# First scores ahead of the last natural values, gate weights beside the ring, values' first chunks split during the gates

## The chip, the cores and the metric

The kernel runs on one core of one Trainium2 chip. The metric is the device time of one execution, in microseconds. Three executions of the kernel before took 2294.04 to 2295.73 us, median 2295.2.

## The reference, cut to what matters

All arithmetic is float32. A first block runs 256 tokens of width 1024 through two layers. Each projects the normalised tokens and feeds four kinds of attention of four heads each: stick-breaking (`sb`), block attention with a relative bias (`mb`), a native sparse attention of three branches (`cmp` on 15 compressed blocks, `slc` and `win`) with sigmoid gates, and differential attention (`df`). A second block adds 256 context tokens, a matrix LSTM and a latent attention of eight heads, each followed by a convolutional feed-forward. Cut to what the change touches:

```
proj = rmsnorm(x) @ w_in                       # queries, keys ("proj"); values, gates ("nat")
kc, vc = (gelu(blocks(t) @ w1) @ w2 for t in (k_c, v_c))    # "hid": the hidden rows of the compression
for each head unit: o = softmax(q @ k.T * scale + bias) @ v
o_nsa = g0 * o_cmp + g1 * o_slc + g2 * o_win;  x = x + concat(o) @ w_out
...
x_m = h @ w_up; x_c = silu(dwconv(x_m)); gates = x_c @ w_gates + b; v = x_m @ w_v   # mLSTM
q = rope(rms(h @ w_dq) @ w_uq); o = softmax(q @ k.T * s) @ v @ w_out                # latent attention
```

## The kernel before, in words

Every engine has an instruction list written out by hand, and semaphores tie them. One list of 1 MB slots (128 x 2048 floats) holds all large weights in their order of use. SyncE loads them into a ring of two slots (`load`, `load_span`); slot w is issued when `slot_done` counts w - 1, that is when the slot before the last has been split.

A product in float32 is made of three products of rounded parts. ScalarE copies a slot of weights into the rounded type (L1309, two halves), VectorE subtracts to get the rest (L1789, two halves, `slot_done`). The same is done to each chunk of 128 input rows (L1333 or L1331 on ScalarE, L1814 or L1811 on VectorE). TensorE then does three products for each output tile (`linear`, L793; L798 where the input is stationary, "natural"). `feed_to(q)` splits all chunks up to q and the weight slots that they need, and one slot ahead; `ws` holds two split slots and `xs` four 256-column cells. So ScalarE and VectorE stay a little ahead of TensorE. Where one of them has other work in its list at that time, TensorE waits.

Results go to eight PSUM banks, given out in turn by `ticket_plan`. A ticket waits until the copy of the ticket eight turns before has freed its bank (`bank_free`).

**Attention of the first block, in each of the two layers.** After the projections, TensorE does the first six of eight natural chunks, the hidden rows of the compression (L943, 128 small products), the last two natural chunks, and four small transposes (L953). Then comes a loop over p = 0 to 15, a pipeline of three steps. In step p TensorE does the scores of pair p (L1005, L1007; 14 pairs of head units), one or two units of the modulation (L965), the transposes of the weights of pair p - 2 (L1048; L1044 for `cmp`) and their products with the values (L1077, L1079). VectorE makes the logits and their maxima (L1945 to L1948; L1936, L1938 for `sb`) and normalises pair p - 1 (L2012 to L2025, which releases the transposes). ScalarE takes the exponentials (L1464, L1465; L1448 to L1454 and L1470 for `sb`) and copies the transposed weights out (L1442). In layer 0 eight transposes of the context tokens (L1031) stand in each of the steps 0 and 1, and ScalarE copies them out (L1475). The natural results are copied out by ScalarE (L1411 to L1415) ahead of the loop; TensorE's scores of pairs 1 and 2 take the banks that these copies free. At p = 0 VectorE makes the gelu's argument (L1953 to L1963), ScalarE its exponential at p = 1 (L1427), VectorE the rest (L1979 to L1983). At p = 7 (`OUT_X_AT`) ScalarE and VectorE split the first four chunks and the second weight slot of the output projection. The loop ends in `linear(out)`.

**mLSTM.** Four groups `m_up` end in the convolution and its silu, then 32 products for the gates (L1127, straight from the ring slot, not split), then 14 filler products on constants (`keep_warm`, L866), then four groups of values `m_v` (16 chunks each, natural). VectorE adds the gates' bias (L2106, L2108, which also counts `slot_done`), ScalarE makes a logarithm of the sigmoid (L1568 to L1572), and VectorE runs six scans (L2122 to L2126) with chunks of the first group fed between them. When the scans' result is ready, four transposes (L1138) follow the first group, and ScalarE copies them out (L1587) behind that group's four results (L1583).

**Latent attention.** In a loop over i, one of 16 score tiles each (L1238, L1239), TensorE transposes tile i - 2 (L1247) and multiplies with the values for each head (L1257). VectorE rotates two heads' queries in each of the first four steps (L2345 to L2348), which frees the banks that the score tiles take, reduces the maximum (L2381) and normalises the tile before (L2387, L2389, which releases the transposes). At i = 1 it splits the first slot of the output projection.

Of the kernel before, what the change touches and what calls it, by code (L numbers as in the profile page):

```python
# [42 lines left out]
OUT_X_AT = 7  # L43
# [92 lines left out]
NP = NU // 2  # L136

# [111 lines left out]
def stream_plan():  # L249
# [11 lines left out]
    w.direct("m_gates")  # L261
# [22 lines left out]
def ticket_plan():  # L284
# [3 lines left out]
    for l in range(DEPTH):  # L288
# [6 lines left out]
        n.add(("hid", l))  # L295
        n.add(("hidT", l))
        for p in range(NP + 2):
            if p < NP:
                n.add(("S", l, 2 * p), 1)
                n.add(("S", l, 2 * p + 1), 1)  # L300
# [3 lines left out]
            if l == 0 and p < 2:  # L304
                n.add(("xC", 2 * p))
                n.add(("xC", 2 * p + 1))
# [89 lines left out]
def G(*name):  # L396
    return ST.g[name if len(name) > 1 else name[0]]
# [13 lines left out]
def build(nc, tokens, stream, side, params, params1, consts, onehot, out, scratch):  # L411
    with ExitStack() as ctx:
# [109 lines left out]
        mv = region(o("v"), (4, MH * T2))  # L522
        mqk = region(o("qk"), (4, T2))
# [36 lines left out]
        late_full = [sem(f"late_side_full{i}") for i in range(2)]  # L560
        conv_ready = sem("conv_ready")
# [110 lines left out]
        def _(sp):  # L672
# [77 lines left out]
            load_span(at, ST.n)  # L750
# [8 lines left out]
        def _(pe):  # L759
# [156 lines left out]
            for l in range(DEPTH):  # L916
# [29 lines left out]
                linear(G("nat", l), 6)  # L946
# [7 lines left out]
                ins.then_inc(bank_full[n % BANKS], 1)  # L954

                for n in range(N(("proj", l, 1)), N(("proj", l, 1)) + 4):
                    pe.wait_ge(bank_free[n % BANKS], n // BANKS + 1)
# [31 lines left out]
                for p in range(NP + 2):  # L989
                    if p < NP:  # L990

                        two = [(UNITS[i], N(("S", l, i))) for i in (2 * p, 2 * p + 1)]
                        if two[0][0]["kind"] == "cmp":
                            for n in (N(("kc", l)), N(("vc", l))):
                                pe.wait_ge(bank_free[n % BANKS], n // BANKS + 1)
                        for u, n in two:
                            pe.wait_ge(bank_free[n % BANKS], n // BANKS)
                        for t in range(2):
                            for u, n in two:
                                f = slice(u["r"], u["r"] + u["kk"])  # L1000
                                rows_q = qk[f, u["q"], t * P:t * P + P]
                                if u["kind"] == "cmp":
                                    ins = mm(ps(n, 16 * t, 16 * t + 16), rows_q, kcT[f, :], start=True, stop=True)
# [4 lines left out]
                                if t == 1:  # L1008
                                    ins.then_inc(bank_full[n % BANKS], 1)
# [1584 lines left out]
```

## Time and profile before

| | |
|---|---|
| median of three executions | 2295.2 us |
| profiled execution | 2294.72 us, span 2292.9 us |
| TensorE busy, of the span | 2210.5 us (96%) |
| VectorE, ScalarE busy | 1340.3 us (58%), 1183.8 us (52%) |
| mean granted TensorE clock | 0.99 of 2.4 GHz |
| read from memory | 309.11 MB, 135 GB/s |

PE is TensorE's products and PEld its weight loads, DVE is VectorE, ACT ScalarE, SPq SyncE's queue. A timeline row gives start and duration in us, engine, line, operation, output and inputs, how many, and in brackets the idle time of the engine before and what ended it. Durations of pipelined products overlap, and some records can be missing. In rows of windows each engine has its busy time and its number of instructions, then come the granted clock (1.00 is 2.4 GHz, 0.50 is 1.2 GHz), the DMA share and GB/s.

### The profile page before, as it was taken

What the parts mean: (1) busy time and instruction counts of PE and PEld (TensorE: products, weight loads), DVE (VectorE), ACT (ScalarE), POOL (GpSimd) and SP (SyncE); (2) the same over time, 40 slices, a digit from 0 to 9 for tenths busy, and PEclk for the clock granted to TensorE, in tenths of its full rate; (3) what the DMA queues carried; (4) which work ended last, traced back from release to release, by engine and by line L of the source; (5) the groups of instructions that cost most, each with busy time, mean ns of one, the idle gap of its engine ahead of it and who ended that gap; (6) DMA issues with size and microseconds to landing.
All of it is one profiled execution on the core that took longest, in us unless ns stands there. A gap on an engine that the chain in (4) does not pass through costs nothing.

```text
span 2292.9 us, 33613 instructions
## 1 busy us (share of the span) xinstructions
PE 2210.5 (96%) x13542; PEld 1831.2 (80%) x13542; DVE 1340.3 (58%) x2204; ACT 1183.8 (52%) x2002; POOL 0.2 (0%) x4
## 2 busy tenths in 40 slices
PE   8989999979999999999999999999999998999998
PEld 8659989849999777787677676868888877668998
DVE  6776645685654655445667664356666436546764
ACT  4665535575544564444344443257555337447764
POOL 0000000000000000000000000000000000000000
PEclk9999999989999999999999999999999999899999
DMA  8735575753576213222222121222222222214542
GB/s 311 269 134 182 216 302 201 281 199 120 178 291 258 92 56 110 92 92 92 74 74 70 68 83 37 92 74 92 97 106 92 92 92 92 92 42 154 182 168 99
DMA packets 45719, 312.28 MB, mean 136 GB/s; under 512 B 4951, under 2 KB 7255, under 8 KB 8580
## 3 DMA queue, kind: packets, MB, share of 16 engines
q1 hardware_dynamic: 45572, 310.20, 37.3%
q8 instruction: 107, 1.75, 0.3%
q14 instruction: 40, 0.33, 0.0%
HBM read 309.11 MB, written 1.07 MB: 135 GB/s over the span
## 4 chain that ended last, share of the span: by engine, by line
PE 84%; DVE 9%; ACT 5%; issue 1%; DMA 0%; ACTq 0%; DVEq 0%; SPq 0%
PE bank L793 63%; PE bank L798 9%; DVE ws L1789 2%; PE bank L965 2%; ACT ws L1309 2%; PE bank L1195 1%; DVE xs L1814 1%; PE bank L1166 1%; PE bank L1239 1%; DVE hT L1945 1%; PE bank L1257 1%; PE bank L1238 1%; PE bank L866 1%; PE bank L1127 1%; DVE arena L2216 1%
## 5 line engine op out<-in xcount | busy, mean ns | idle before, releaser
L793 PE MATMUL bank<-xs,ws 128*128 128x256 f32 (+1 forms) x9648 | 1569.0, 323 | 26.5 <-DVE xs L1814 15.3
L793 PEld LDWEIGHTS bank<-xs,ws 128*128 128x128 f32 x9648 | 1396.5, 190 | 204.3 <-issue 34.1
L1789 DVE TENSOR_TENSOR ws<-ring,ws 128x1024 fp32r<-128x1024 f32 x462 | 545.5, 1222 | 293.3 <-ACT ws L1309 293.2
L1309 ACT ACTIVATE ws<-ring 128x1024 fp32r<-128x1024 f32 x462 | 462.7, 1049 | 300.3 <-PE bank L793 195.0
L1814 DVE TENSOR_TENSOR xs<-arena,xs 128x512 fp32r<-128x512 f32 (+1 forms) x286 | 162.5, 581 | 287.2 <-ACT xs L1333 285.8
L1333 ACT ACTIVATE xs<-arena 128x512 fp32r<-128x512 f32 (+1 forms) x286 | 149.2, 539 | 332.4 <-PE bank L793 221.8
L798 PE MATMUL bank<-ws,xs 128*128 128x512 f32 (+1 forms) x1008 | 230.0, 388 | 5.7 <-ACT arena L1587 2.2
L798 PEld LDWEIGHTS bank<-ws,xs 128*128 128x128 f32 x1008 | 188.5, 189 | 45.8 <-DVE ws L1789 2.6
L1333 ACT ACTIVATE xs<-hT 128x512 fp32r<-128x512 f32 (+1 forms) x216 | 123.0, 573 | 196.9 <-PE bank L793 187.9
L1814 DVE TENSOR_TENSOR xs<-hT,xs 128x512 fp32r<-128x512 f32 (+1 forms) x216 | 133.5, 620 | 155.5 <-ACT xs L1333 155.4
L1811 DVE SCALAR_TENSOR_TENSOR xs<-xT,par,xs 128x256 fp32r<-128x256 f32 x112 | 51.2, 480 | 11.9 <-ACT xs L1331 11.8
L1331 ACT ACTIVATE xs<-xT,par 128x256 fp32r<-128x256 f32 x112 | 51.9, 495 | 7.3 <-DVE xT L1829 7.3
L965 PE MATMUL bank<-arena,cs 128*32 128x256 f32 x768 | 55.5, 409 | 0.0
L1343 ACT ACTIVATE arena<-xT 128x512 f32<-128x512 f32 (+1 forms) x52 | 28.5, 563 | 36.5 <-DVE xT L2267 26.7
L1537 ACT ACTIVATE arena<-bank,par 128x512 f32<-128x512 f32 (+1 forms) x60 | 41.6, 693 | 9.9 <-PE bank L793 9.9
L866 PE MATMUL bank<-con 128*128 128x256 f32 x202 | 46.4, 382 | 0.0
L866 PEld LDWEIGHTS bank<-con 128*128 128x128 f32 x202 | 38.2, 192 | 8.0 <-issue 3.2
L1195 PE MATMUL bank<-arena 128*128 128x512 f32 (+1 forms) x128 | 42.7, 488 | 0.1
L2076 DVE SCALAR_TENSOR_TENSOR arena<-arena,par 128x510 f32<-128x510 f32 (+1 forms) x60 | 38.9, 648 | 3.3 <-ACT arena L1556 3.3
L2078 DVE SCALAR_TENSOR_TENSOR arena<-arena,par 128x510 f32<-128x510 f32 (+1 forms) x60 | 39.2, 653 | 2.1
L1048 PE MATMUL bank<-con,hT 128*128 128x128 f32 x144 | 24.1, 302 | 15.3 <-DVE hT L2025 12.6
L1195 PEld LDWEIGHTS bank<-arena 128*128 128x128 f32 x128 | 24.1, 190 | 18.3 <-issue 15.3
(259 smaller groups left out, 1364.3 us busy)
## 6 DMA issues: line engine op xcount, KB each, us to landing
ring<-in_stream SPq DMA_DIRECT2D x233, 1024.0 KB, 4.8
arena<-in_side SPq DMA_DIRECT2D x56, 1024.0 KB, 5.0
arena<-bias_vectors SPq DMA_DIRECT2D x1, 1536.0 KB, 9.0
hT<-in_tokens SPq DMA_DIRECT2D x1, 1024.0 KB, 5.0
arena<-in_tokens SPq DMA_DIRECT2D x1, 1024.0 KB, 12.7
out<-arena SPq DMA_DIRECT2D x2, 512.0 KB, 3.1
arena<-in_params SPq DMA_DIRECT2D x1, 918.0 KB, 8.2
arena<-bias_vectors SPq DMA_DIRECT2D x1, 706.0 KB, 10.5
```

The lines of the kernel that those rows point to most:

```text
L793: ins = mm(ps(n, c, c + g.T), a[wi][:, p * P:(p + 1) * P], x[xi], start=first, stop=last)
L798: ins = mm(ps(n, 0, width), x[xi][:, (p // nh) * P:(p // nh + 1) * P], a[wi][:, (p % nh) * 512:(p % nh) * 512 + width], start=first, stop= ...
L866: mm(ps(n, at, at + cols), ones, con[:, 0:cols], start=True, stop=True)
L965: ins = mm(bank[n % BANKS][c:c + 32, 0:T], cs[:, k, 2 * ADA_B - 2 - 2 * u:2 * ADA_B + 30 - 2 * u], wd[:, k, :], start=(u == 0 and k < 4), ...
L1195: ins = mm(ps(n, T_AT[st_], T2), mv[:, st_, h * T2 + e * P:h * T2 + (e + 1) * P], mP[:, 0, OFF[st_]:OFF[st_] + T2 - T_AT[st_]], start=(st_ ...
L1309: do(ws[:, i % 2, 0, c], ring[:, w % R, c], ACT.Copy).then_inc(w_high, 2 // halves_in)
L1331: do(split_x(q, 0), source(g, k), ACT.Identity, scale=par_at(g.gain, k)).then_inc(x_high, 1)
L1333: do(split_x(q, 0), source(g, k), ACT.Copy).then_inc(x_high, 1)
L1537: return do(dst, ps(n, 0, cols), ACT.Identity, scale=w[:, 1:2], bias=b)
L1789: ins = v.tensor_tensor(ws[:, i % 2, 1, c], ring[:, w % R, c], ws[:, i % 2, 0, c].bitcast(F32), ALU.subtract)
L1811: stt(split_x(q, 1), source(g, k), par_at(g.gain, k), split_x(q, 0).bitcast(F32), ALU.mult, ALU.subtract).then_inc(x_done, 1)
L1814: v.tensor_tensor(split_x(q, 1), source(g, k), split_x(q, 0).bitcast(F32), ALU.subtract).then_inc(x_done, 1)
```

## The change

In the attention loop the scores of pair 0 move ahead of the last two natural chunks, and the four small transposes go between these two chunks. ScalarE takes the exponentials of pair 0, of lambda and of the gelu ahead of the natural copies. The gates of the sparse attention are finished at VectorE's step 3 in place of step 1. The context's transposes move from steps 0 and 1 to 1 and 2. `OUT_X_AT` becomes 14. In the mLSTM the gates' weights leave the stream: a DMA of 1 MB brings them into a free part of the arena once `m_up` group 0 is done; it stands in SyncE's list between the loads of the stream. ScalarE and VectorE split chunks 0 and 1 of the first values (and the slot after) ahead of their work on the gates, the 14 fillers go, and the transposed gate rows are copied out ahead of the first group's results. In the latent attention VectorE's split of the output projection's first slot moves from i = 1 to i = 6.

```diff
-OUT_X_AT = 7
+OUT_X_AT = NP                                   # 14
-    w.direct("m_gates")                         # stream_plan
@@ ticket_plan
         n.add(("hid", l))
+        n.add(("S", l, 0))
+        n.add(("S", l, 1))
         n.add(("hidT", l))
         for p in range(NP + 2):
-            if p < NP:
+            if 0 < p < NP:
...
-            if l == 0 and p < 2:
-                n.add(("xC", 2 * p))
+            if l == 0 and 1 <= p <= 2:
+                n.add(("xC", 2 * p - 2))
@@ sync
-            load_span(at, ST.n)
+            load_span(at, ST.w[("m_up", 2)])
+            n = N(("m_up", 0), 3)
+            sp.wait_ge(bank_full[n % BANKS], n // BANKS + 1)
+            sp.dma_start(gate_weights, side[DEPTH * SIDE_W]).then_inc(gates_full, 16)
+            load_span(ST.w[("m_up", 2)], ST.n)
@@ tensor
-                linear(G("nat", l), 6)
+                for n in range(N(("proj", l, 1)), N(("proj", l, 1)) + 4):
+                    pe.wait_ge(bank_free[n % BANKS], n // BANKS + 1)
+                scores(0)                       # the score products of step p, now a function
+                linear(G("nat", l), 6, 7)
                 n = N(("hidT", l))
...
                     ins = nc.tensor.transpose(ps(n, 16 * i, 16 * i + 16), hrow[:, i, :], ident[0:16, 0:16])
                 ins.then_inc(bank_full[n % BANKS], 1)
+                linear(G("nat", l), 7)
...
-            pe.wait_ge(slot_full[(W("m_gates")) % R], 16 * ((W("m_gates")) // R + 1))
-            wd = slot(W("m_gates"), MK)
+            pe.wait_ge(gates_full, 16)
+            wd = gate_weights.rearrange("p (k n) -> p k n", k=MK)
...
-            keep_warm(N("m_aT"), T, T, 14)
@@ scalar
                 feed(G("nat", l))
+                for i in range(2):
+                    softmax_exp(i)              # waits logits_ready; the two Exp of a pair's unit
+                act_.wait_ge(lam_sum, seen(lam_sum))
+                do(lam[:, 2:4], lam[:, 0:2], ACT.Exp).then_inc(lam_exp, 1)
+                act_.wait_ge(gelu_arg, l + 1)
+                do(hid, hidg, ACT.Exp, scale=-2.0 * math.sqrt(2.0 / math.pi)).then_inc(gelu_exp, 1)
                 n = N(("rT", l))
                 ...                             # the natural copies, as before
-                    if p < NP:
+                    if 0 < p < NP:
...
             exp_ln_tables()
+            feed_to(G("m_v", 0).q0 + 1)
             act_.wait_ge(bank_free[N("m_gates") % BANKS], N("m_gates") // BANKS + 1)
...
             for h in range(MH):
+                if h == 0:
+                    feed(G("m_v", h), 1)
+                    ...                         # the copy of m_aT, moved here from behind the four copies
                 feed(G("m_v", h), 2)
@@ vector
+                logits(0)
+                ...                             # hidT, gelu argument, lambda, gelu: from steps 0 and 1
+                for p in range(NP + 1):
+                    if 0 < p < NP:
+                        logits(p)
...
+                    if p == 3:
+                        ...                     # gates: wait gate_exp, + 1, reciprocal, from step 1
@@
+            feed_to(G("m_v", 0).q0 + 1)
             n = N("m_gates")
             dve.wait_ge(bank_full[n % BANKS], n // BANKS + 1)
-            v.tensor_scalar(grow[0:64, 0, :], ..., ALU.add).then_inc(slot_done, 1)
+            v.tensor_scalar(grow[0:64, 0, :], ..., ALU.add)
@@
             for i in range(2 * AH + 1):
-                if i == 1:
+                if i == 6:
                     weights_to(G("a_out").s0)
```

## Rows read from the trace of the kernel before

**Rows 1.** The page: the chain that ended last, by engine.

```profile
PE 84%; DVE 9%; ACT 5%; issue 1%; DMA 0%; ACTq 0%; DVEq 0%; SPq 0%
```

**Rows 2.** Waits of PE: total us, times, longest us.

```profile
PE bank L1048 <- DVE hT L2025: 12.6, 9, 6.0
...
PE bank L1044 <- DVE hT L2025: 5.9, 4, 2.6
...
PE bank L1077 <- ACT hT L1442: 5.8, 8, 0.9
```

**Rows 3.** Timeline, second layer, start of the attention loop.

```profile
448.28 5.18 PE L798 MATMUL bank<-ws,xs 128*128 128x512 f32 x24
...
451.80 0.69 ACT L1411 ACTIVATE arena<-bank,arena 128x512 f32<-128x512 f32 x1 [4.96 <-PE bank L798]
...
454.77 0.56 DVE L1945 SCALAR_TENSOR_TENSOR hT<-bank,arena 128x384 f32<-128x384 f32 x1 [5.18 <-PE bank L1007]
...
457.00 0.21 DVE L1953 COPY arena<-bank 128x64 f32<-128x64 f32 x1
...
462.19 0.17 DVE L2012 RECIPROCAL arena<-arena 128x4 f32<-128x4 f32 x1
...
463.00 1.54 PE L1048 MATMUL bank<-con,hT 128*128 128x128 f32 x6 [6.03 <-DVE hT L2025]
...
469.52 0.88 PE L1048 MATMUL bank<-con,hT 128*128 128x128 f32 x6
```

**Rows 4.** Timeline, first layer, the same stretch.

```profile
91.17 1.46 PE L1031 MATMUL bank<-con,arena 128*128 128x128 f32 x8
```

**Rows 5.** Windows: busy time of PE, PEld, DVE, ACT, POOL, then clock.

```profile
463.00:479.00 16.00, 14.66 (x122) 8.45 (x122) 11.36 (x31) 12.08 (x31) 0.00 (x0) 0.75 0.42 142
...
493.30:501.60 8.30, 5.72 (x47) 2.58 (x44) 7.17 (x29) 4.85 (x19) 0.00 (x0) 0.81 0.91 374
...
501.60:518.60 17.00, 13.91 (x118) 8.41 (x118) 14.91 (x52) 12.70 (x44) 0.00 (x0) 0.89 0.01 2
...
135.00:150.40 15.40, 12.37 (x118) 7.40 (x115) 14.82 (x53) 13.14 (x44) 0.00 (x0) 1.00 0.02 6
...
871.00:873.00 2.00, 2.00 (x6) 1.52 (x6) 1.97 (x4) 0.00 (x0) 0.00 (x0) 0.50 0.88 373
...
1988.00:1996.00 8.00, 8.00 (x16) 3.20 (x16) 6.72 (x18) 2.53 (x6) 0.00 (x0) 0.50 0.00 0
```

**Rows 6.** Timeline, second layer, behind the split for the output projection.

```profile
490.36 2.36 DVE L1789 TENSOR_TENSOR ws<-ring,ws 128x1024 fp32r<-128x1024 f32 x2 [0.42 <-ACT ws L1309]
...
497.09 0.66 PE L1044 MATMUL bank<-con,hT 128*16 128x128 f32 x4 [2.58 <-DVE hT L2025]
```

**Rows 7.** Timeline, second layer, end of the loop.

```profile
520.11 0.87 ACT L1442 ACTIVATE hT<-bank 128x384 f32<-128x384 f32 x2 [1.79 <-PE bank L1048]
...
531.27 0.75 DVE L2036 SCALAR_TENSOR_TENSOR arena<-arena,stat 128x512 f32<-128x512 f32 x1 [12.67 <-ACT stat L1369]
```

**Rows 8.** Timeline, mLSTM, the gates and the first values.

```profile
847.39 13.89 PE L1127 MATMUL bank<-arena,ring 128*128 128x512 f32 x32
...
861.32 0.74 DVE L2106 TENSOR_SCALAR arena<-bank,par 64x512 f32<-64x512 f32 x1 [8.60 <-PE bank L1127]
...
869.17 45.84 PE L798 MATMUL bank<-ws,xs 128*128 128x512 f32 x192 [1.84 <-DVE ws L1789]
...
887.51 27.08 PEld L798 LDWEIGHTS bank<-ws,xs 128*128 128x128 f32 x120 [0.54 <-DVE xs L1814]
...
919.84 10.49 PE L798 MATMUL bank<-ws,xs 128*128 128x512 f32 x45 [2.18 <-ACT arena L1587]
```

**Rows 9.** Timeline, latent attention, first steps.

```profile
1980.60 2.35 DVE L1789 TENSOR_TENSOR ws<-ring,ws 128x1024 fp32r<-128x1024 f32 x2
...
1984.31 2.04 PE L1238 MATMUL bank<-arena 128*128 128x512 f32 x2 [2.51 <-DVE arena L2348]
...
1997.37 0.66 PE L1247 MATMUL bank<-con,arena 128*128 128x128 f32 x4
```

More of the change, by code:

```diff
@@ L989, in _ @@
                 for p in range(NP + 2):
-                    if p < NP:
[L992 to L1003, printed above, removed]
-                                elif t == 0:
-                                    ins = mm(ps(n, 0, 128), rows_q, qk[f, u["k"], 0:128], start=True, stop=True)
-                                else:
-                                    ins = mm(ps(n, 128, 384), rows_q, qk[f, u["k"], :], start=True, stop=True)
-                                if t == 1:
-                                    ins.then_inc(bank_full[n % BANKS], 1)
+                    if 0 < p < NP:
+                        scores(p)
                     if p == CMP_AT:
@@ L1023, in _ @@
                         ins.then_inc(bank_full[n % BANKS], 1)
-                    if l == 0 and p < 2:
+                    if l == 0 and 1 <= p <= 2:
                         pe.wait_ge(dma_ctx, 16)
-                        for j in (2 * p, 2 * p + 1):
+                        for j in (2 * p - 2, 2 * p - 1):
                             n = N(("xC", j))
@@ L1470, in _ @@
                             do(sbuf[:, j % 6, :], sbuf[:, j % 6, :], ACT.Exp).then_inc(sb_ready, 1)
-                    if l == 0 and p < 2:
-                        for j in (2 * p, 2 * p + 1):
+                    if l == 0 and 1 <= p <= 2:
+                        for j in (2 * p - 2, 2 * p - 1):
                             n = N(("xC", j))
@@ L1927, in modulation_out, with logits @@
                     dve.wait_ge(dve_own, own(dve_own))
-                for p in range(NP + 1):
-                    two = (2 * p, 2 * p + 1)
-                    for i in two if p < NP else ():
+                def logits(p):
+                    for i in (2 * p, 2 * p + 1):
                         u, s, n = UNITS[i], sbuf[:, i % 6, :], N(("S", l, i))
@@ new lines, in _ @@
+                dve.wait_ge(dve_own, own(dve_own))
+                v.tensor_scalar(lam[:, 5:6], lam[:, 4:5], -lam_init, None, ALU.add)
+                dve.wait_ge(gelu_exp, l + 1)
+                v.tensor_scalar(hid, hid, 1.0, None, ALU.add).then_inc(dve_own, 1)
+                dve.wait_ge(dve_own, own(dve_own))
+                v.reciprocal(hid, hid).then_inc(dve_own, 1)
+                dve.wait_ge(dve_own, own(dve_own))
+                v.tensor_tensor(hidg, hid, gx, ALU.mult).then_inc(hid_ready, 1)
@@ L2025, in _ @@
                                 v.tensor_scalar(s[:, w:end], s[:, w:end], st[:, j, 5:6], None, ALU.mult).then_inc(p_ready, 1)
+                    if p == 3:
+                        dve.wait_ge(gate_exp, seen(gate_exp))
+                        v.tensor_scalar(lam[:, 16:40], lam[:, 16:40], 1.0, None, ALU.add).then_inc(dve_own, 1)
+                        dve.wait_ge(dve_own, own(dve_own))
+                        v.reciprocal(lam[:, 16:40], lam[:, 16:40]).then_inc(dve_own, 1)
+                        dve.wait_ge(dve_own, own(dve_own))
+                        gates = lam[:, 16:40].rearrange("p (a b) -> p a b", a=2)
                     if p == OUT_X_AT:
```

108 lines of the change are left out of this document (53 added, 55 removed).

## The prediction

> **What bounds the kernel now.** I read the page's chain first: 84% of the span is TensorE itself, 9% VectorE, 5% ScalarE [rows 1]. So a change that leaves TensorE's work alone can only win where TensorE waits, or where its clock is low. The view of TensorE's waits comes next: the longest, 6.0 us, is for the first weights of the attention loop, 5.9 us in all go to the transposes of the compressed branch, 5.8 us to ScalarE's copies of transposed weights [rows 2]. The timeline of the loop's start shows why. In the second layer the last natural chunks begin at 448.28 as the hidden products end, VectorE idles 5.18 us until pair 0's scores at 454.77, and TensorE then waits until 463.00 [rows 3]; the first layer is alike with a shorter wait, since the context's transposes (1.46 us for the second eight) fill part of it [rows 4]. The windows give the clock: 0.75 behind the 6 us wait, 0.81 around the wait in the middle of the loop, 0.50 in the first values and for at least eight microseconds of the latent attention [rows 5]. Each low stretch follows a wait of TensorE, so a wait that goes takes more than its own length with it.
>
> **The change part by part**, all against the profiled execution's 2294.72 us (span 2292.9 and 1.8 outside it; the median of the three runs is 0.5 above).
>
> *a. Start of the loop, second layer.* Nothing is added on TensorE, the order changes. The four hidden transposes and pair 0's scores take 1.3 us (448.28 + 5.18 = 453.46 to 454.77), so with the scores first VectorE begins its logits by 449.7 in place of 454.77. A pair's logits take 2.2 us (454.77 to 457.00) and end at 451.9, hidden by chunk 6 (2.6 us, half of 5.18). The hidden transposes come at 452.2, between chunks. From 457.00 to 462.19 lie pair 1's logits (2.2) and all small operations (3.0), of which I give the gelu's argument 1.2: ready at 453.5. ScalarE does the gelu's exponential (0.3) and only then the natural copies, which began at 451.80 before. That wait is new, and behind it stand the copies that free the banks of pair 1's scores: three copies of at most 0.69 us, pipelined some 1.4, so 455.3. TensorE is through chunk 7 at 454.9: a wait of 0.5. Scores of pair 1 (0.9) 456.3, logits to 458.2, and 0.8 from the reciprocal to the transposes (462.19 to 463.00): 459.0. **4.0 us** earlier than 463.00. The step after took 6.5 us (463.00 to 469.52), at a mean clock of 0.75 over this stretch. With no long wait ahead of it the clock should be full and the step take 4.5: **2.0 us**, between 0 and 2.
>
> *b. Start of the loop, first layer.* The same 4.0, but sixteen transposes of the context, up to 1.5 us for eight, now stand between pair 1's scores and the first weights' transposes, in place of beside VectorE's logits. That makes TensorE the bound: 1.5 us later, so 2.5 gained; and the compression's products wait for the banks of the context's copies, which stand behind ScalarE's 3 us of stick-breaking work. So of the step after I take 0.3 only. **2.8 us**, between 1 and 5.
>
> *c. The split for the output projection, each layer.* At step 7 VectorE does 2.36 us of weights and four chunk rests of 0.4: 3.9 us, and ScalarE 3.4. VectorE fills 14.82 of 15.40 us in the first layer's later steps [rows 5], so it can't catch up; TensorE waits 2.58 us at 497.09 [rows 6] and 0.9 for ScalarE's copies ahead of it [rows 2]. These **3.4 us** go. In step 14 VectorE has 12.67 us of idle time for it. ScalarE does not: its 3.4 us now stand ahead of the copies of the last transposes, where it was idle 1.79 us [rows 7]. So these come 1.6 late, the value products 1.3 after a little slack, and with them the projection: 1.3 back. The ring: SyncE had both later slots of the projection in it since step 8; now the second is ordered 8 us ahead of its use with 5 us to land, so nothing. Net **2.1 us per layer, 4.2**, between 0 and 6.8. In the second layer the low clock goes with the wait: the means 0.81 over 8.3 us and 0.89 over 17.0 make 3.2 + 3.7 = 6.9 us at half rate, 3.4 us lost if TensorE were the bound in all of it; I take three quarters: **2.6 us**, between 0 and 3.4.
>
> *d. Gates and first values.* The gates' products end at 847.39 + 13.89 = 861.28, the first values start at 869.17 [rows 8]: 7.9 us, in which the 14 fillers stand. With chunks 0 and 1 and two weight slots split beforehand (about 7 us on either engine, beside 13.9 us of products for which both are idle: VectorE 8.6 us of it) the values follow at once. VectorE's rests end about 861.8, half a microsecond after it would have taken up the bias. From bias over logarithm and three scans to chunk 2 are 7.2 us: 869.0. TensorE is through two chunks (120 loads in 27.08, so 2.71 each) at 866.7: a new wait of 2.3. Chunk 6 then starts 18.9 us after the gates' end (6 chunks 16.3, 2.3, and 0.3 of what it waited before) against 887.51 - 861.28 = 26.2. **7.4 us** if the clock stays, 5.5 if it falls in that new wait as it did after the old one of 1.84 us (0.50 at 871 to 873, 1.9 us lost). I take **6.5**. The added DMA waits in SyncE's list for the first `m_up` group, and behind it a stream slot that is used 11 us later: it is hidden with some 3 us to spare, and costs up to 3 if not. Moving the copy of the gate rows ahead takes away the 2.18 us at 919.84; ScalarE's order makes chunk 2 of the second group 0.8 later: **1.4**.
>
> *e. Latent attention.* VectorE's 2.35 us at 1980.60 go from step 1, and the third score tile, which waits for a rotation behind it, starts at 1981.9 in place of 1984.31 [rows 9]. VectorE is the bound up to its third set of weights, TensorE at its low clock then the bound up to 1997.37. At full clock the latter would start behind VectorE at 1992.8, 4.6 gained; at the low clock 1.6 is left. I take **3.3**. In step 6 VectorE has over 1 us of idle time in each step and TensorE looks ahead two tiles: 0 to 0.3, taken as 0.
>
> Here a rule can be weighed. In the row 1988 to 1996 TensorE is busy 8.00 of 8.00 us and the clock stays at 0.50; these are score products of one or half a set of rows. The Trainium skill, "TensorE: Matmul & The Clock Gate", section "What's actually happening", has a busy TensorE at 2.4 GHz. By that rule part e would give its whole 4.6; the row disagrees. The same section calls the gate's window free-running and its cost run-variable; no row here shows that.
>
> Sum: 4.0 + 2.0 + 2.8 + 4.2 + 2.6 + 6.5 + 1.4 + 3.3 = 26.8. 2294.7 - 26.8 = 2267.9, by the median **2268**.
>
> **The rivals.**
> *The loop takes the start back (18%).* The loop's later steps are VectorE's (14.82 of 15.4 us busy), and the natural copies behind the gelu hold ScalarE. Then only VectorE's idle time shrinks, about 2 us a layer for a and b (4.8 less), and of c nothing stays (6.8 less): 26.8 - 11.6 = 15.2, **2280**. Against it: TensorE, not VectorE, is late in the 6.5 us step, and 3.4 us of waits stand right after the split.
> *The low clock moves and does not go (17%).* The waits left (2.3 before values' chunk 2, 1.3 at the end of each loop, the stick-breaking step) each can bring it down. Without the clock's share in a (2.0), c (2.6), d (1.0) and e (1.7): 7.3 less, **2275**.
> *All falls go (10%)*, also those at the stick-breaking steps (about 1 us each) and in d and e: 1.9 + 0.9 + 1.3 more, **2263**.
> *Slower: the gates' products don't hold the clock (2%).* The fillers go, and a TensorE that is busy with such products stays at 0.50 in the last row of rows 5. If the same held from the gates on, the 16 chunks of the first group (43.4 us) would run at half the rate: 43 us more, against 26.8: **2311**. It decides from 27 us of such loss, ten chunks. Against it: in the values of before the clock fell too and was back by 887.51, from where the loads come at 0.226 us each.
>
> **How the numbers follow.** Forecast 53%, own range 2264 to 2273. The range 2260 to 2281 takes in the three faster rivals and part of the bounds of b and c (some 8% lie outside above, 7% below). What can be told from no change is 0.2%, 4.6 us. Every case but the last is faster by more; small remainders of the first rival with a DMA that is late could come to no change: faster 0.96, same 0.02, slower 0.02.
>
> **What would show it.** In the changed profile: VectorE's first logits some 1.5 us behind the hidden products, a wait of the first L1048 group under 1 us; no wait of over 1 us at the transposes of the second compressed pair; a wait of about 1.3 us ahead of the last value products; the first values right behind L1127 and a wait of 2 us two chunks later; the second score tile pair of the latent attention without 2.5 us of wait. The prediction is wrong if the transposes of pair 0 come later than 12 us after the hidden products, if the ring's loads show up ahead of the output projection or of `m_up` group 2, or if the granted clock in the values is below 1 for more than one short stretch.

## The result and the profile after

The changed kernel takes **2264.7 us** (median of 4 runs, 2263.8 to 2266.2) where the kernel before took 2294.6 (4 runs): ratio 0.9871, 95% interval 0.9854 to 0.9888, so 29.9 us less. The forecast was 2268. A second set of runs on another occasion gave 2265.8 against 2292.3, ratio 0.9884 (0.9863 to 0.9904). The profiled executions have spans of 2262.1 and 2292.9 us: 30.8 to explain. Below, a "fall" is a stretch of some microseconds in which the granted clock goes from 2.4 GHz to 1.2 GHz and back (1.00 and 0.50 in the rows; a window that holds only part of one shows a value between).

The page of the changed kernel: the chain by engine, which answers to [rows 1].

```profile
PE 83%; DVE 10%; ACT 5%; issue 1%; DMA 0%; ACTq 0%; DVEq 0%; SPq 0%
```

TensorE is still the bound. Its waits (total us, times, longest), against [rows 2]:

```profile
PE bank L1090 <- ACT hT L1463: 5.9, 8, 0.9
PE bank L834 <- ACT arena L1355: 3.4, 5, 1.2
PE bank L1061 <- DVE hT L2041: 4.5, 9, 0.8
PE bank L1061 <- ACT hT L1489: 2.9, 3, 1.3
```

The weights' transposes (L1048 before, L1061 now) wait 4.5 us for VectorE in place of 12.6; the longest is 0.8 in place of 6.0. Those of the compressed branch (L1044, now L1057) wait 0.35 us where they waited 2.58. The timeline of the second layer's start, against [rows 3] (start, length, engine, line; in brackets the idle time before and its releaser):

```profile
441.75 0.84 PE L951 MATMUL bank<-arena 128*16 128x128 f32 x24
442.52 0.49 PE L969 MATMUL bank<-arena 64*128 64x128 f32 x4
443.87 0.56 DVE L1966 SCALAR_TENSOR_TENSOR hT<-bank,arena 128x384 f32<-128x384 f32 x1
447.75 0.26 ACT L1431 ACTIVATE arena<-arena 128x64 f32<-128x64 f32 x1 [0.45 <-DVE arena L1985]
447.91 0.67 ACT L1437 ACTIVATE arena<-bank,arena 128x512 f32<-128x512 f32 x1
450.29 0.56 DVE L1966 SCALAR_TENSOR_TENSOR hT<-bank,arena 128x384 f32<-128x384 f32 x1 [1.20 <-PE bank L971]
453.33 1.01 PE L1061 MATMUL bank<-con,hT 128*128 128x128 f32 x6 [0.83 <-DVE hT L2041]
457.80 0.87 PE L1061 MATMUL bank<-con,hT 128*128 128x128 f32 x6
462.38 0.96 PE L1061 MATMUL bank<-con,hT 128*128 128x128 f32 x6 [1.34 <-ACT hT L1489]
```

The hidden products end at 442.59. VectorE's logits begin 1.3 us later, the exponential of the gelu stands ahead of the natural copies, and the first transposes start 10.74 us behind the end of the hidden products, where they started 14.65 behind (463.00 - 448.35). The next step takes 4.47 us, as forecast. The end of the loop, against [rows 7]:

```profile
500.61 0.88 PE L1061 MATMUL bank<-con,hT 128*128 128x128 f32 x6
502.42 0.86 ACT L1463 ACTIVATE hT<-bank 128x384 f32<-128x384 f32 x2
503.42 0.65 PE L1090 MATMUL bank<-hT,arena 128*64 128x256 f32 x4 [0.94 <-ACT hT L1463]
505.70 2.54 PE L801 MATMUL bank<-xs,ws 128*128 128x256 f32 x19 [0.50 <-ACT arena L1511]
```

From the last transposes to the projection's third chunk it is 5.09 us, before 4.10 (523.62 - 519.52): the 1.0 us that the split gives back. The gates and the values, against [rows 8], with the end of the last `m_up` group ahead of them:

```profile
820.42 2.36 DVE L1810 TENSOR_TENSOR ws<-ring,ws 128x1024 fp32r<-128x1024 f32 x2 [0.26 <-ACT ws L1321]
824.88 5.73 PE L801 MATMUL bank<-xs,ws 128*128 128x512 f32 x24 [0.67 <-DVE xs L1835]
830.45 13.89 PE L1140 MATMUL bank<-arena 128*128 128x512 f32 x32
843.78 6.04 PE L806 MATMUL bank<-ws,xs 128*128 128x512 f32 x24
844.38 0.74 DVE L2130 TENSOR_SCALAR arena<-bank,par 64x512 f32<-64x512 f32 x1 [2.13 <-PE bank L1140]
851.55 38.79 PE L806 MATMUL bank<-ws,xs 128*128 128x512 f32 x168 [1.73 <-DVE xs L1835]
890.27 0.46 PE L1150 MATMUL bank<-con,arena 64*128 64x64 f32 x4
```

The values follow the gates at once and a wait of 1.73 us comes two chunks later. New, and not forecast, is the wait of 0.67 us at 824.88: before, no wait stands in the last 27.5 us ahead of the gates. The windows of the changed kernel (columns as in [rows 5], the clock is the number ahead of the last two):

```profile
128.00:143.30 15.30, 12.27 (x114) 7.61 (x118) 14.74 (x53) 13.12 (x46) 0.00 (x0) 1.00 0.08 34
453.30:469.80 16.50, 14.92 (x160) 8.95 (x160) 15.37 (x48) 14.88 (x44) 0.00 (x0) 1.00 0.77 284
843.80:867.00 23.20, 21.35 (x92) 16.86 (x91) 15.68 (x21) 8.30 (x12) 0.00 (x0) 1.00 0.25 88
1955.40:1967.10 11.70, 8.45 (x25) 3.06 (x25) 11.04 (x30) 3.36 (x9) 0.00 (x0) 1.00 0.01 1
2167.20:2171.20 4.00, 3.96 (x20) 3.97 (x21) 3.89 (x11) 1.85 (x6) 0.00 (x0) 0.57 0.61 242
```

The clock is 1.00 in the second layer's loop, in the values and in the latent attention, and 0.57 at one place where it had been full before: behind a wait in the last feed-forward. In the first layer one fall is left (clock 0.67 from 104.8 to 109.9 us), where the kernel before had two, from 99 and from 109 us on. Where the 30.8 us came from, by the starts of the same instruction in both traces (gain since the mark above; the last column is what experiments 5, 6 and 9 below show to be the clock's in this pair of executions):

```
mark                                    before     after    gain   clock
output projection, first layer          155.40    149.67    5.73    1.6
output projection, second layer         523.62    505.70   12.19    6.1
gates' products                         847.39    830.45   -0.98    0
products behind the first values        914.94    890.27    7.73    0.6
last group ahead of latent attention   1967.19   1940.57    1.95    0
projection behind latent attention     2045.92   2013.53    5.77    3.5
end                                     2292.9    2262.1    -1.6   -1.4
sum                                                        30.8   10.4
```

### The profile page after: what moved, and what is told of

It reads as the page before. It is cut to its first block, busy times and chain, and to the rows that moved or that the text cites. A ratio compares the mean times of both kernels' runs of the same rounds, so it can differ in the third digit from the quotient of the medians.

```text
span 2262.1 us, 33558 instructions
## 1 busy us (share of the span) xinstructions
PE 2190.6 (97%) x13514; PEld 1819.1 (80%) x13514; DVE 1340.1 (59%) x2204; ACT 1182.6 (52%) x2002; POOL 0.2 (0%) x4
## 4 chain that ended last, share of the span: by engine, by line
PE 83%; DVE 10%; ACT 5%; issue 1%; DMA 0%; ACTq 0%; DVEq 0%; SPq 0%
PE bank L801 63%; PE bank L806 8%; DVE ws L1810 2%; ACT ws L1321 2%; PE bank L1207 2%; PE bank L996 1%; DVE xs L1835 1%; PE bank L1178 1%; DVE hT L1966 1%; PE bank L874 1%; PE bank L1269 1%; PE bank L1140 1%; DVE arena L2239 1%; PE bank L1251 1%; ACT xs L1345 1%
## 5 line engine op out<-in xcount | busy, mean ns | idle before, releaser
L874 PE MATMUL bank<-con 128*128 128x256 f32 x174 | 40.1, 381 | 0.0
L874 PEld LDWEIGHTS bank<-con 128*128 128x128 f32 x174 | 32.8, 192 | 6.8 <-issue 2.7
L996 PEld LDWEIGHTS bank<-arena,cs 128*32 128x32 f32 x768 | 20.2, 110 | 16.0 <-issue 4.8
```

The lines of the kernel that those rows point to most:

```text
L874: mm(ps(n, at, at + cols), ones, con[:, 0:cols], start=True, stop=True)
L996: ins = mm(bank[n % BANKS][c:c + 32, 0:T], cs[:, k, 2 * ADA_B - 2 - 2 * u:2 * ADA_B + 30 - 2 * u], wd[:, k, :], start=(u == 0 and k < 4), ...
```

## The experiments

Experiments 1 to 4, 7 and 8 are edits of the changed kernel, 10 is one of experiment 8's, 9 is one of the kernel before, and 5 and 6 have none; every ratio is against the kernel before. The first four undo one part each.

**1. The split for the output projection back at step 7.**

```diff
-OUT_X_AT = NP
+OUT_X_AT = 7
```

> The changed kernel with the split for the output projection back at step 7 (part c undone). Theory: a layer loses the 3.16 us of waits in the middle of the loop again and wins back the 1.0 us at its end, so 2.2 us a layer; in the second layer the wait of 2.6 us takes the clock down behind it, as before, another 2.5: the output projection starts 2.2 us later in the first layer and 6.9 (4.4 if the clock stays) in the second, the whole 4.4 to 6.9 longer: about 2269 to 2271.5, with 1.5 us either way from falls further on that move. Rival (VectorE is the bound in the later steps whatever the place of the split): the projection starts within 0.5 us of the changed kernel in both layers.

2268.2 us, just under the 2269 to 2271.5 expected; ratio 0.9895 (0.9878 to 0.9913); span 2266.1. The timeline of both layers around the wait:

```profile
126.30 0.66 PE L1057 MATMUL bank<-con,hT 128*16 128x128 f32 x4 [2.57 <-DVE hT L2041]
131.11 1.54 PE L1061 MATMUL bank<-con,hT 128*128 128x128 f32 x6
...
487.04 0.66 PE L1057 MATMUL bank<-con,hT 128*16 128x128 f32 x4 [2.57 <-DVE hT L2041]
490.40 1.00 PE L1061 MATMUL bank<-con,hT 128*128 128x128 f32 x6 [0.27 <-DVE hT L2041]
```

The wait is back in both layers, and both projections come later: 4.7 us in the first layer and 2.2 in the second. That is 3.15 for the wait less 1.0 at the end in each, and 2.5 for the clock in one. (Counted from each layer's first transposes and against experiment 2, which up to there is the changed kernel without a fall: 58.17 us against 53.48, and 54.52 against 52.37.) But it is the other layer: the six transposes behind the wait take 1.54 us in the first layer and 1.00 in the second, where in the kernel before the clock fell in the second only. The rival (VectorE is the bound anyway) is refuted.

**2. The split for `a_out` back at step 1.**

```diff
-                if i == 6:
+                if i == 1:
                     weights_to(G("a_out").s0)
```

> The changed kernel with the split of the first weights of a_out back at step 1 of the latent attention (part e undone). Theory: the wait of 2.5 us at the second pair of score tiles comes back (2.0 to 2.4 us net) and with it the low clock of some 8 us (2.3 more): the last feed-forward starts 4.3 to 4.7 us later; whether the later fall behind the tenth step (1.3 us in the kernel before) comes back depends on where the waits fall. Total about 2269. Rival 1: the split is hidden and the whole 5.8 us of gain came from waits that fell elsewhere in time: the feed-forward starts at the same time within 0.5 us. Rival 2: the wait comes back but the clock stays at full: 2.0 to 2.4 us, 2267.

2266.1 us, ratio 0.9883 (0.9866 to 0.9899); span 2264.2. The timeline shows the wait back, 2.51 us:

```profile
1956.41 1.10 PE L1250 MATMUL bank<-arena 128*128 128x512 f32 x2 [2.51 <-DVE arena L2371]
```

The window of the 12 us behind it has a clock of 0.57, with TensorE busy in 11.89 of them:

```profile
1956.40:1968.40 12.00, 11.89 (x20) 4.04 (x20) 10.22 (x27) 3.31 (x8) 0.00 (x0) 0.57 0.21 83
```

The later fall came too (5.66 us from the last wait for VectorE to the last products with the values, 3.98 at full clock). From the last group ahead of the latent attention to the projection behind it it takes 77.90 us in place of 72.96, 4.9 more: 3.3 up to that later fall, 1.7 in it. The place of the split is the cause of the wait, which at full clock is worth 2.3 us (75.24 in experiment 6 against 72.96); the first fall then cost about 1 us and not the 2.3 expected. At full clock TensorE waits 0.61, 0.56, 0.67 and 0.65 us for VectorE right behind the wait (experiment 6); at low clock it has no such waits, since VectorE is nearly as late. The median lies only 1.4 us above the changed kernel's and below both expectations (2269 and 2267): this execution has neither of the two falls of the changed kernel's first profile, and a total doesn't tell the two sorts of loss apart.

**3. The 14 fillers back between gates and values.**

```diff
+            keep_warm(N("m_aT"), T, T, 14)
             linear(G("m_v", 0))
```

> The changed kernel with the 14 fillers put back between the gates' products and the first values. Theory (they were pure cost, the gates' products keep the clock up by themselves): 6.2 us of fillers in series, of which the wait of 1.73 us ahead of chunk 2 is taken back: the values' seventh chunk starts 4.5 us later, clock 1.0 in both kernels; total 2269. Rival (the fillers do hold the clock for what follows): the chunks behind them run faster than in the changed kernel and less than 3 us is lost. Rival (a wait remains behind them): 6.2 us lost, 2271.

2268.7 us, ratio 0.9897 (0.9879 to 0.9915); span 2263.4. TensorE's timeline, and then the window around it:

```profile
842.86 6.21 PE L874 MATMUL bank<-con 128*128 128x256 f32 x28
848.72 44.33 PE L806 MATMUL bank<-ws,xs 128*128 128x512 f32 x192
892.98 0.46 PE L1151 MATMUL bank<-con,arena 64*128 64x64 f32 x4
```

```profile
829.00:900.00 71.00, 70.46 (x284) 52.45 (x283) 38.95 (x50) 33.09 (x50) 0.00 (x0) 1.00 0.18 63
```

From the gates' start to the products behind the first values it takes 4.0 us more (892.98 - 829.13 = 63.85 against 59.82), with the clock at 1.00 in both: the fillers were cost alone, and the clock is full behind the gates' products without them. The sum missed 0.5 us: behind the fillers the 192 products of the group run in one piece, so they cover a little more than the wait of 1.73.

**4. The start of the loop as before, in both layers** (scores of pair 0 behind the last natural chunk, natural copies ahead of the first exponentials; all hunks of the diff in the attention but the place of the split).

```diff
-                scores(0)
-                linear(G("nat", l), 6, 7)
+                linear(G("nat", l), 6)
...
-                    if 0 < p < NP:
-                        scores(p)
+                    if p < NP:
+                        scores(p)
```

> The changed kernel with the start of both layers' loops as before (parts a and b undone: first scores after the last natural chunk, natural copies ahead of the first exponentials), all else kept. Theory: the parts add up: 3.6 us lost in the first layer; in the second 3.9 at the first weights' transposes, 2.0 in the step after (clock 0.75 again) and 1.6 in the stick-breaking step if the clock falls there again: 9.5 to 11.1 us, about 2274 to 2276. Rival (the loop's later steps took part of it back, so c gained less than it shows): the projection of the second layer starts less than 8 us later than in the changed kernel (both layers together), with longer waits of TensorE in steps 6 to 13 of the changed kernel than here.

2273.3 us, ratio 0.9917 (0.9900 to 0.9935); span 2270.3. The wait of 6.03 us stands at 459.20, and the second layer's projection starts 8.7 us later than in experiment 2, whose loop is the changed kernel's without a fall (513.12 against 504.40): 3.3 from the first layer, of which 1.3 is a fall, 3.9 from the wait and 1.56 from one fall in the second. Behind the stick-breaking step both kernels need the same 43.3 us (469.80 to 513.12; 461.07 to 504.40). So nothing of the start is taken back by the later steps, which was the first rival of the prediction. The 8.7 us lie below the 9.5 to 11.1 expected: the upper end had a fall in the stick-breaking step, which did not come, and under the lower end are 0.3 us in the first layer and 0.4 in the step behind the first transposes. (Against the changed kernel's own first profile, which has a fall in the first layer, it is 7.4 us.)

**5. The changed kernel again, and 6. the kernel before again**, both without an edit.

> The changed kernel itself, unchanged, profiled once more. Theory (after a wait of TensorE the clock falls or stays by where the wait falls in a rhythm that is not tied to the kernel): every wait has the same length as in the first profile, but the low stretches lie elsewhere, 1.4 to 1.6 us each; where the clock is full, the two lists of starts run parallel within 0.1 us. Rival (the fall belongs to the wait): the clock falls again at 106 to 110 and at 2168 to 2171 us and nowhere else.

> The kernel before, unchanged, profiled once more. Theory of a rhythm not tied to the kernel: its waits of 6.0, 3.2 and 2.6 us come again at the same instructions, with low stretches that are not all the same: of the seven in the first profile some are missing, others are new; the span differs by up to 4 us from 2292.9. Rival (the fall belongs to the wait): the same seven, the span within 0.5 us.

2265.8 us (2265.2 to 2266.4), span 2264.7, and 2291.1 us (one run), span 2289.3. The timeline of the changed kernel's second profile, then the timeline and the window of the one before:

```profile
1965.42 1.90 PE L1250 MATMUL bank<-arena 128*128 128x512 f32 x2 [0.65 <-DVE arena L2371]
...
2171.35 6.12 PE L801 MATMUL bank<-xs,ws 128*128 128x256 f32 x48 [1.98 <-DVE xs L1835]
```

```profile
1984.20 1.10 PE L1238 MATMUL bank<-arena 128*128 128x512 f32 x2 [2.51 <-DVE arena L2348]
```

```profile
1984.00:1996.00 12.00, 8.58 (x25) 3.20 (x26) 11.28 (x32) 3.47 (x9) 0.00 (x0) 1.00 0.23 85
```

The same wait of 1.98 us in the last feed-forward was followed by 48 products in 7.51 us in the first profile (clock 0.57) and by the same 48 in 6.12 now. The same wait of 2.51 us in the latent attention left the clock at 0.50 [rows 5] and at 1.00 here; the stretch up to the next projection took 78.73 us in the one and 75.24 in the other. Falls came at 106 us again and new at 464 and 1965 us, the last behind nothing longer than 0.67 us. So at these places execution decides, and not the kernel alone. It is not so everywhere: of the eight falls of the kernel before ahead of its last 10 us, six came again at the same instructions, and only the two of the latent attention did not. At the long waits ahead of the first transposes (3.2 us in the first layer, 6.03 in the second) the clock fell in all three profiles that have them (before, experiments 4 and 6); at the 2.6 us in the middle of a loop it fell in three cases of six, at the 1.34 us of the first layer's stick-breaking step in five profiles of nine and at that of the second layer in three. The Trainium skill, "TensorE: Matmul & The Clock Gate", section "What's actually happening", calls the gate's window free-running and the cost of the slow start of a kernel run-variable; that falls at one and the same wait come and go agrees with it. The spread of the kernel before fits too: in one set of seven runs 2286.3 us at a mean clock of 0.997 and 2295.6 at 0.989.

**7. The values' first weight slot split one step later.**

```diff
-        def follows(s_):
+        def follows(s_, last):                                  # last: the group's last chunk
...
-            return s_ + 1 < len(ST.split) and ST.split[s_ + 1][0] == ST.split[s_][0] + 1
+            return (s_ + 1 < len(ST.split) and ST.split[s_ + 1][0] == ST.split[s_][0] + 1
+                    and (last or s_ + 1 != G("m_v", 0).s0))
...                                                             # both callers pass it
```

> The changed kernel, in which the first weight slot of the values' first group is split behind the last chunk of m_up group 3 in place of behind its second-last chunks' split (the look-ahead to that slot waits for the last chunk). Theory (the 1.0 us lost in m_up group 3 comes from VectorE splitting this slot, 2.36 us, ahead of two taps and the last chunks' rests): TensorE's wait of 0.67 us in the group's last chunks goes and the gates' products start 1.0 us earlier, with the wait of 1.73 us before chunk 2 unchanged; 1.0 us faster than the changed kernel in equal stretches. Rival (the loss comes from the gates' weights' transfer or from the ring): the wait stays.

2263.5 us, ratio 0.9873 (0.9853 to 0.9894); span 2262.0. The wait at 824.88 is gone, the last 120 products run in one piece, and chunk 2 of the values starts 48.44 us behind the first of these 120 in place of 49.42 (TensorE's timeline):

```profile
802.16 27.50 PE L802 MATMUL bank<-xs,ws 128*128 128x512 f32 x120 [0.68 <-DVE xs L1836]
...
850.60 38.80 PE L807 MATMUL bank<-ws,xs 128*128 128x512 f32 x168 [1.74 <-DVE xs L1836]
```

The 0.98 us are won back. The cause: with the gates' slot out of the stream, the look-ahead in `feed_to` (`follows`) sees the values' first slot next to the last of `m_up` and puts 2.36 us of split between VectorE's taps.

**8. Three things more**: the late slot; ScalarE's split of the projection's chunks 2 and 3 behind its last copies; fillers in three waits.

```diff
                     if p == OUT_X_AT:
-                        feed_to(G("out", l).q0 + 3, False)
+                        feed_to(G("out", l).q0 + 1, False)
+                        weights_to(G("out", l).s0 + 1)
+                    if p == NP + 1:
+                        feed_to(G("out", l).q0 + 3, False)
...
+                            if p == SB_STEP and j == 2 * p - 4:
+                                keep_warm(n, 0, T, 2)
...
-            linear(G("m_v", 0))
+            linear(G("m_v", 0), 0, 2)
+            keep_warm(N("m_aT"), T, T, 3)
+            linear(G("m_v", 0), 2)
```

> The changed kernel with three things more: the late slot; in step 14 of the loop ScalarE leaves the split of the projection's chunks 2 and 3 (0.7 us) until it has copied the last transposes; and fillers inside waits that are there anyway, 2 (0.9 us) in the wait of 1.34 us of the stick-breaking step of each layer and 3 (1.36 us) in the wait of 1.73 us before the values' chunk 2. Theory: late slot 1.0; the wait of 0.94 us ahead of the last value products shrinks by 0.5 in each layer; the fillers cost nothing and no fall comes at the three waits that they fill: 2.0 us faster than the changed kernel in stretches at full clock, and 0 to 1.6 more where that one fell; median about 2262. Rival: the projection's chunks 2 and 3 come late and the projection stands 0.5 or more later, which takes the gain of the loop's end back: 1.0 us faster only; or the fillers delay the stick-breaking step's transposes (they end 0.4 us before the data is there by the sum): then up to 0.5 us slower there.

2260.9 us, ratio 0.9863 (0.9842 to 0.9883); span 2259.1, 4.9 us less than the changed kernel in the same set of runs. The fillers cost nothing: the stick-breaking step's transposes stand 9.04 us behind the first ones, in the changed kernel 9.05. The change of ScalarE's order disappoints, as the timeline of the second layer's end shows:

```profile
502.18 0.65 PE L1094 MATMUL bank<-hT,arena 128*64 128x256 f32 x4 [0.33 <-ACT hT L1469]
...
504.92 0.50 PE L803 MATMUL bank<-xs,ws 128*128 128x256 f32 x2 [0.97 <-ACT arena L1520]
```

The wait for the copies shrinks from 0.94 to 0.33, the next one for ScalarE's norm grows from 0.50 to 0.97: 0.15 us a layer, the rival's case. So 1.3 us come from the order. The rest of the 4.9 is put down to falls: the mean clock of these runs is 0.999 to 1.000, that of the changed kernel's 0.996 to 0.997. One fall came all the same, in the first layer from 100 us on, behind a wait of 1.20 us that was not filled.

**9. The kernel before with its waits filled.**

```diff
                             u, n = UNITS[j], N(("PT", l, j))
+                            fill = {0: (6, 12)[l], 4: 2, 14: 5}.get(j, 0)
+                            if fill:
+                                keep_warm(n, 0, T, fill)
...
-            keep_warm(N("m_aT"), T, T, 14)
+            keep_warm(N("m_aT"), T, T, 17)
```

> The kernel before, with its order of work unchanged, and fillers (0.45 us each, products that nobody reads) only inside waits of TensorE that are there anyway: 12 in the wait of 6.0 us at the second layer's first weights' transposes and 6 in that of 3.2 us in the first layer, 2 in each stick-breaking step's wait of 1.34 us, 5 in each wait of 2.6 us at the second compressed pair, 3 more behind the 14 ahead of the values. It measures the clock's share of the gain alone. Theory (about a third of the gain is the clock's): all waits and the order stay, the low stretches of the loop and of the values go: 6.1 us in the second layer (2.0, 1.6 and 2.5), 1.6 to 3 in the first, about 1.9 in the values: 9 to 11 us less than the first profile of before, some 2284. The latent attention is not filled and can still fall. Rival (the long waits, not the clock, make up the gain; a clock that falls costs little since VectorE is the bound then): less than 3 us.

2284.9 us, ratio 0.9961 (0.9947 to 0.9974), 8.9 less than the kernel before in the same set (9 to 11 expected, less than 3 by the rival); span 2283.1. TensorE's timeline, second layer:

```profile
459.93 1.00 PE L1051 MATMUL bank<-con,hT 128*128 128x128 f32 x6 [0.27 <-DVE hT L2028]
...
476.40 0.66 PE L1047 MATMUL bank<-con,hT 128*16 128x128 f32 x4 [0.35 <-DVE hT L2028]
...
490.40 0.66 PE L1047 MATMUL bank<-con,hT 128*16 128x128 f32 x4 [0.22 <-DVE hT L2028]
...
514.47 5.30 PE L793 MATMUL bank<-xs,ws 128*128 128x256 f32 x42 [0.51 <-ACT arena L1495]
```

Work and order are those of before, and no product starts earlier than its data. Yet from the first transposes to the compressed pair it takes 16.47 us in place of 20.09 (463.00 to 483.09), and from the second compressed pair to the projection 24.07 in place of 26.53: 6.1 us that were only clock. The first of these stretches takes 16.48 us in the changed kernel (453.33 to 469.81), the same to 0.01. The first layer gives 3.2 more, the gates and values 0.6 (66.92 against 67.55; expected 1.9). In the latent attention, which was not filled, the clock fell here.

**10. More fillers in experiment 8's kernel**: one ahead of each of the first three transposes of the latent attention, three and two in the last feed-forward.

```diff
+                    if j < 3:
+                        keep_warm(n, 0, T, 1)
                     pe.wait_ge(ap_ready, seen(ap_ready))
...
+                    if l and i == 5:
+                        keep_warm(N(("ffn_in", 1, 5)), 0, T, 3)
                     linear(G("ffn_in", l, i))
+                if l:
+                    keep_warm(N(("ffn_out", 1)), 0, T, 2)
```

> The combined kernel (e8) with fillers in more waits: one of 0.45 us in each of the three waits of 0.6 us ahead of the first transposes of the latent attention, 3 in the wait of 1.98 us ahead of the last feed-forward's sixth group, 2 in that of 1.3 us ahead of its second matrix. Theory: no fall is left but at the wait of 1.2 us of the first layer; the profile shows at most one low stretch ahead of the last 10 us, and the runs lie within 1.5 us of each other at 2259 to 2261. Rival: the fillers push the score tiles or the group's start back; then the latent attention or the last feed-forward is 0.3 to 1 us longer than in e8 at full clock.

**2259.6 us** (2259.3 to 2260.2, ratio 0.9854, 0.9838 to 0.9869), span 2257.5: the lowest time here, 34 us under the kernel before in its set, though the interval of the ratio overlaps with experiment 8's. No low stretch is left ahead of 2248 us, and the runs lie within 0.9 us. From the first wait of the latent attention to the last matrix's second part it takes 225.92 us, in experiment 8 225.94: the new fillers cost nothing, but in this pair of profiles they won nothing either, since the clock was full here in both. Of the 1.6 us between the two spans 1.5 are there before the latent attention begins: 1.1 of these are experiment 8's fall in the first layer, behind the wait of 1.20 us, which is unfilled here too and had no fall. That the new fillers keep the clock up is therefore not shown. In the timeline the wait of 1.98 us shrinks to 0.69:

```profile
2164.21 6.12 PE L803 MATMUL bank<-xs,ws 128*128 128x256 f32 x48 [0.69 <-DVE xs L1850]
```

## Why the prediction came out right, step by step

The order of the work gave 20.4 us and the clock 10.4; the prediction had 19.5 and 7.3 (2.0, 2.6, 1.0 and 1.7, as its second rival counts them). The mechanisms that it names are the ones that the traces show, but that the sum came so close is partly luck: it is the net of misses both ways, the largest +2.5 in part e, and -1.4 and -1.0 for two losses that it had not foreseen. With experiment 6's execution as the one before, in which the clock stayed up in the latent attention, e would have given 2.3 in place of 5.8. Its signs held: first logits 1.3 us behind the hidden products, a first wait of 0.83 us, 0.35 at the second compressed pair, 1.73 two chunks into the values, 0.24 at the latent attention's third score tile; the wait at the end of the loop is 0.94 where it said 1.3.

- **a.** The first transposes 4.0 us earlier: 3.9. The step after, 2.0 from the clock: 2.05. Its main sum left out the stick-breaking step, 1.6 us more from the clock (experiment 9); the third rival has it, at about 1 us.
- **b.** 2.8 forecast, 3.6 seen, of which 1.6 is a fall: both executions of before had two in this layer, this one had one. By the order alone it is 2.0: 3.1 at the first transposes (97.69 to 94.60), less 1.1 lost behind them: from there to the projection it takes 54.54 us in experiment 9 and 53.48 in experiment 2, neither with a fall, a gain of 1.1 where part c alone gives 2.2. The step had 2.5 at the first transposes, which TensorE now reaches without a wait, so it is the bound there as the step says. The mis-sized term is the next one, +0.3 forecast and -1.1 seen: the wait for the banks of the context's copies, which the step names, is 1.20 us long.

```profile
99.34 0.59 PE L1028 MATMUL bank<-arena 128*128 128x16 f32 x4 [1.20 <-ACT xT L1494]
```

- **c.** 2.1 a layer net: 2.16 and 2.15 (3.15 won, 1.0 given back; 3.4 and 1.3 forecast). The clock in the second layer: 2.46, forecast 2.6. Experiment 1 shows the cause; there the clock fell in the first layer, in both executions of before in the second.
- **d.** 7.4 with the clock up, 6.5 taken: 7.7, of which 0.6 is the clock (experiment 9). The step let VectorE's rests end at 861.8, half a microsecond too late for the bias, but its own terms don't give this: about 7 us of work in 8.6 us of VectorE's idle time would end before the gates do. VectorE was idle 2.13 us ahead of the bias and took it up right behind the gates, and so the wait of 2.3 was 1.73. The copy of the gate rows: 1.4 forecast, 1.7 seen. The gate weights' DMA was hidden.
- **e.** 3.3 forecast, 5.8 seen, 2.3 of it by the order. The step took a mean of full and low clock; here the execution of before was low in two places and that of after in none. Of the 4.6 us that it gives for the full clock up to 1997.37, 4.46 were seen (30.18 us from 1967.19 against 25.72); the later fall, which it does not price, is the rest.
- **What it missed:** the look-ahead that now crosses from `m_up` to the values (-1.0, experiment 7), and the fall in the last feed-forward (-1.4), where nothing had been changed. "The low clock moves" was a rival for all its places together; the profiles show places that fall in one execution and not in the next, each for itself, so that rivals 2 and 3 are rather the two ends of one spread than cases.
- **The rivals:** the loop that takes the start back is refuted by experiments 1 and 4, the slower case by experiment 3 and by the changed kernel's own windows.
- **Its model of the clock** ("each low stretch follows a wait, so a wait that goes takes more than its own length with it") holds at the waits of 3 and 6 us, in every profile that has them, and on average only elsewhere: behind one and the same shorter wait the clock fell or not, and it also fell where there were only waits of 0.2 to 0.67 us, close together.

## What to carry to other kernels

Before a gain is read off two traces, list the low-clock stretches of both and cost them apart: they were a third of it here, and some belong to the execution and not to the kernel. A second profile of each kernel shows which. Waits of TensorE that can't be removed can be filled with products that nobody reads, here up to about 0.3 us less than the wait, which delayed nothing: that alone gave 9 us to the kernel before. The 14 between two stages, which stood mostly outside a wait, cost 4.0 us (experiment 3). When a slot is taken out of a weight stream, look at every rule that asks whether two slots are neighbours; the work that a look-ahead pulls forward lands on an engine that had other things queued.

## What the runs showed of the hardware

- The granted clock after one and the same wait differs between executions. The 1.98 us in the last feed-forward: low in two profiles (the changed kernel's first, experiment 9), full in nine. The 2.51 us in the latent attention: low in three (before, experiments 2 and 9), full in one (experiment 6). The 6.03 and 3.2 us ahead of a loop's first transposes: low in all three that have them (before, experiments 4 and 6).
- A fall can come without a long wait: in experiment 5 at 1965 us the longest wait of the stretch was 0.67 us.
- A TensorE that is busy throughout can stay low: 11.89 of 12.00 us busy in the window of experiment 2, clock 0.57; 6.98 of 7.00 in experiment 5, clock 0.51.
- A fall can cost much less than half its length where another engine is close behind: the 12 us at 0.57 in experiment 2 could have cost 5 us and cost about 1 (3.3 us lost up to there, of which the wait at full clock is 2.3). In the kernel before, the same place cost 1.8 (3.49 less 1.68 for the later fall).
